# A decoder layer with a 32-expert mixture: three blocks of the first expert picked by TensorE instead of one or two, the routing tables built behind them, and the output projection's weights loaded in two halves

## What is computed

```python
xn = rms_norm(h, norm1_gain)
h = h + hybrid_mixer(xn, w_in, ...)              # ends in concatenate([h_m, h_g]) @ w_out
hn = rms_norm(h, norm2_gain)
logits = hn @ w_router + b_router
top_logit, top_idx = top_k(logits, 4)
gate = softmax(top_logit)
# for every expert e and each of its tokens:
hb = hn[tok] @ w_up[e] + b_up[e]                 # w_up[e] is 1024 x 2048
h_glu, h_lin = split(hb, 2)
h_glu = minimum(h_glu, 7); h_lin = clip(h_lin, -7, 7)
act = h_glu * sigmoid(1.702 * h_glu) * (h_lin + 1)
y[tok] += gate * (act @ w_down[e] + b_down[e])   # w_down[e] is 1024 x 1024
out = rms_norm(h + y, final_gain)
```

## Time and profile before

| | |
|---|---|
| median of three executions | 1283.21 us |
| the profiled execution: its time | 1281.32 us |
| the profiled execution: its span | 1279.5 us |
| TensorE matmuls busy | 1120.3 us, 88% |
| VectorE / ScalarE / GpSimd busy | 499.5 / 201.8 / 217.7 us |
| moved by DMA | 473.00 MB, 370 GB/s over the span |
| granted TensorE clock, mean | 0.951 of 2.4 GHz |

### The profile page before, as it was taken

The page is one execution under the profiler, slowest core; times in us unless marked ns, Lnnn a source line. Parts: engine busy times, 40 slices in busy tenths (PEclk is TensorE's granted clock), DMA queues, the critical chain, the costliest instruction groups (busy, mean ns, idle before and its releaser), DMA issues.

```text
span 1279.5 us, 28226 instructions
## 1 busy us (share of the span) xinstructions
PE 1120.3 (88%) x11061; PEld 508.3 (40%) x11062; DVE 499.5 (39%) x1234; ACT 201.8 (16%) x293; POOL 217.7 (17%) x385
## 2 busy tenths in 40 slices
PE   9999999989899888899989797989898979797750
PEld 5445554444344333334434343434343434343320
DVE  1393454673333342333333232333333323232317
ACT  2104321112111111111111111111111111111101
POOL 1000112001212221212222121212121212121112
PEclk9999999999999998989999898989898989898985
DMA  9308307669999999999999999999999999999996
GB/s 345 133 33 290 104 5 298 280 257 400 424 434 397 430 429 431 427 428 427 433 426 434 424 429 430 429 428 431 428 433 429 427 430 427 431 425 429 429 414 247
DMA packets 55636, 473.00 MB, mean 370 GB/s; under 512 B 7760, under 2 KB 25484, under 8 KB 41136
## 3 DMA queue, kind: packets, MB, share of 16 engines
q1 hardware_dynamic: 45608, 447.29, 83.6%
q0 software_dynamic: 7776, 20.46, 4.2%
q10 hardware_dynamic: 2216, 4.75, 1.0%
HBM read 447.43 MB, written 25.04 MB: 369 GB/s over the span
## 4 chain that ended last, share of the span: by engine, by line
PE 58%; DMA 34%; DVE 4%; issue 2%; SPq 1%; POOL 0%; ACT 0%; POOLq 0%; DVEq 0%; ACTq 0%
DMA W<-in_w_up_dram 30%; PE B L1601 27%; PE B L1286 11%; PE B L1618 11%; PE B L1441 4%; PE B L1320 2%; DMA hres<-misc,idx_s 2%; DMA yrow<-misc,idx_s 1%; DVE misc L1172 1%; DVE W L1248 1%; SPq L323 1%; DMA W<-in_w_in_dram 0%; DVE W L1249 0%; PE B L1394 0%; PE B L1374 0%
## 5 line engine op out<-in xcount | busy, mean ns | idle before, releaser
L1601 PE MATMUL B<-W,misc 128*32 128x512 f32 x4992 | 583.2, 617 | 108.7 <-DMA W<-in_w_up_dram 84.3
L1601 PEld LDWEIGHTS B<-W,misc 128*32 128x32 f32 x4992 | 183.3, 113 | 462.1 <-issue 454.7
L1618 PE MATMUL B<-W,misc 128*32 128x256 f32 x4992 | 287.7, 381 | 11.4 <-DVE misc L1198 8.7
L1618 PEld LDWEIGHTS B<-W,misc 128*32 128x32 f32 x4992 | 182.3, 111 | 134.7 <-issue 58.1
L1172 DVE TENSOR_TENSOR misc<-B,misc 128x512 f32<-128x512 f32 x77 | 53.3, 692 | 348.5 <-PE B L1601 348.5
L710 ACT ACTIVATE misc<-misc 128x256 f32<-128x256 f32 x78 | 32.5, 416 | 816.8 <-DVE misc L1174 816.8
L1286 PE MATMUL B<-W 128*128 128x512 f32 x320 | 140.2, 593 | 0.0
L526 POOL COPY idx_g<-idx_tab 128x1 uint32 (+1 forms) x77 | 14.3, 186 | 528.6 <-DVE misc L1203 519.6
L710 ACT ACT_TABLE_LOAD x78 | 100.1, 1283 | 5.7 <-DVE order_tab L1150 4.3
L538 POOL DMA_INDIRECT yrow<-misc,idx_s x75 | 75.1, 1001 | 135.0 <-DVE misc L1191 135.0
L1189 DVE TENSOR_TENSOR misc<-B,misc 128x256 f32<-128x256 f32 x78 | 33.1, 425 | 149.0 <-POOL idx_s L534 122.7
(11 more groups left out here) (296 smaller groups left out, 521.5 us busy)
## 6 DMA issues: line engine op xcount, KB each, us to landing
W<-in_w_up_dram SPq DMA_DIRECT2D x56, 4096.0 KB, 33.3
W<-in_w_down_dram SPq DMA_DIRECT2D x28, 4096.0 KB, 30.6
W<-in_w_up_dram SPq DMA_DIRECT2D x16, 2048.0 KB, 15.5
W<-in_w_down_dram SPq DMA_DIRECT2D x8, 2048.0 KB, 18.6
W<-in_w_in_dram SPq DMA_DIRECT2D x5, 2048.0 KB, 16.5
yrow<-W SPq DMA_DIRECT2D x1, 8192.0 KB, 40.4
W<-yrow SPq DMA_DIRECT2D x4, 2048.0 KB, 33.2
W<-in_x_dram SPq DMA_DIRECT2D x8, 512.0 KB, 7.0
```

Source lines behind the costliest of these rows:

```text
L1601: ins = mm(B[0][BT * j:BT * (j + 1), :].rearrange("p (g n) -> p g n", g=2), xT[:, BT * k:BT * (k + 1)], up(par)[:, k, :, QC * j:QC * (j + 1)],
L1618: ins = mm(B[5][BT * j:BT * (j + 1), 0:QC], aT[:, BT * q:BT * (q + 1)], down(par)[:, q, QC * j:QC * (j + 1)], start=(q == 0), stop=(q == N ...
```

## The change

The first `EARLY` = 3 blocks always belong to expert 0 and all have their rows picked by TensorE. Expert 0 is given at least three blocks; block 0 takes tokens of tiles 0 to 2 alone (`Mk_gap` moves tile 3's tokens behind place 31). So block 0 is picked while tile 3 still goes through the router. The up products of blocks 0, 1 and 2 run one after the other, block 1's into bank `B[3]` with its rows in `ysb` (`xT1`), and the small products of the ranks, the order and the token table stand between their `k` steps. The gate table, its spreading and `gate_tab` come behind the third up product, and then the down products of blocks 0 and 1. Filler products (`busy`) fall away. Pieces 2 and 3 of expert 1 are issued by ScalarE's queue instead of SyncE's. `w_out` is loaded in two halves by columns, so that piece 2 of expert 0 can be loaded once tile 3's first half of the projection is done.

```diff
+EARLY = 3
+NBMAX = T * TOPK // BT + NE + EARLY - 1
...
-            sp.dma_start(wo, w_out[0].rearrange("(k p) n -> p k n", p=P)).then_inc(s_wo, 16)
+            for n in range(2):
+                sp.dma_start(wo[n], w_out[0][:, 512 * n:512 * (n + 1)].rearrange("(k p) n -> p k n", p=P)).then_inc(s_wo, 16)
...
+            sp.wait_ge(s_out, 2 * NT - 1)
+            first(0, 2)
             sp.wait_ge(s_out, 2 * NT)
-            first(0, 2)
             first(0, 3)
...
             sp.wait_ge(s_hst, 16 * NT)
-            sp.wait_ge(s_picked, 2)
+            sp.wait_ge(s_picked, EARLY)
             first(0, 4)
-            sp.wait_ge(s_gtab, 1)
-            sp.wait_ge(s_trash, 16)
-            first(1, 2)
-            first(1, 3)
+            sp.wait_ge(s_tab, 1)
...
+            swish(0)
             act.wait_ge(s_ug, 1)
             act.activation(G32, G16, ACT.Copy).then_inc(s_g32, 1)
+            act.wait_ge(m_xg, 16)
+            act.wait_ge(m_u[3], 2)
+            act.wait_ge(s_gtab, 1)
+            for n in (2, 3):
+                load_piece(act, 1, n, slice(1, 2))
...
-            router_turn(NT - 1)
-            router_strips(NT - 1)
-            router_fold(NT - 1)
...
+            router_turn(NT - 1, [0])
             pe.wait_ge(s_pick, 1)
+            early_tile(0)
+            router_turn(NT - 1, [1])
+            early_tile(1)
+            router_strips(NT - 1, [0])
+            early_tile(2).then_inc(s_picked, 1)
+            router_strips(NT - 1, [1])
...
+            def between(g, k):
+
+                if (g, k) == (0, 0):
+                    router_fold(NT - 1)
+                elif (g, k) == (0, 3):
+                    counts()
+                elif (g, k) == (0, 6):
+                    late_rows()
+                elif (g, k) == (1, 4):
+                    order()
+                elif (g, k) == (2, 5):
+                    token_table()
...
-            expert(0, 0, 0, None)
+            block_up(0, 0, 16)
+            place_ranks()
+            pe.wait_ge(s_pick, 2)
+            pick_rows(1, range(NT)).then_inc(s_picked, 1)
+            place_turns()
+            pick_rows(2, range(NT)).then_inc(s_picked, 1)
+            bases()
+            block_up(1, 0, None)
+            block_up(2, 0, None)
+            gate_table()
+            spread_table(1, spread16, tok_s, 4)
+            spread_table(2, spread, gate_s, 6)
+            pe.wait_ge(s_tab, 1)
+            block_down(1, 0, 16)
+            block_down(2, 0, None)
+            more_blocks(0, 0, EARLY, base(1))
```

More of the change, by code:

```diff
@@ L1104, in _ @@
                 .then_inc(s_ranked, 1)
[L1106 to L1111, removed]
+            clamps(0)
+            picked_rows(2)
+            dve.wait_ge(s_place, 1)
+            link(V.tensor_copy(late[0:NE, 2:3], B[6][0:NE, 0:1]))
+            V.tensor_scalar(behind[0:NE, 0:NE + 1], iota_f[0:NE, 0:NE + 1], late[0:NE, 2:3], None, ALU.is_gt)
+            V.tensor_scalar(atp[0:NE, 0:NE], iota_f[0:NE, 0:NE], late[0:NE, 2:3], None, ALU.is_equal).then_inc(s_atp, 1)
+            gated(0)
+            dve.wait_ge(m_act, 1)
+            V.transpose(aT, z[:, 0:256]).then_inc(m_aT, 1)
             link(V.tensor_scalar(bbs[:, 0:NE], B[1][:, 0:NE], float(BT), None, ALU.mult))
@@ L1414, in rank_of @@
             def rank_of(c):
-                for d in range(c + 1):
-                    ins = mm(B[2][:, NE * c:NE * (c + 1)], stri16 if d == c else ones16, Mk16[:, d, :],
-                             start=(d == 0), stop=(d == c))
+                earlier = [(ones16, Mk16[:, d, :]) for d in range(c)]
+                if c == NT - 1:
+                    earlier.append((ones16, Mk_gap))
+                products = earlier + [(stri16, Mk16[:, c, :])]
+                for n, (lhs, rhs) in enumerate(products):
+                    ins = mm(B[2][:, NE * c:NE * (c + 1)], lhs, rhs, start=(n == 0), stop=(n == len(products) - 1))
                 return ins
@@ L1424, in ranks_early @@
                 for c in range(NT - 1):
-                    ins = rank_of(c)
+                    rank_of(c)
+                for d in range(NT - 1):
+                    ins = mm(B[2][:, P:P + 1], ones16, Mk16[:, d, 0:1], start=(d == 0), stop=(d == NT - 2))
                 ins.then_inc(s_cnt, 1)
@@ L1447, in project_out, with router_turn @@
                         cat(c + 1)
-            def router_turn(c):
-                if c >= 1:
-                    pe.wait_ge(s_nTe, 2 * c)
-                for hf in range(2):
+            def router_turn(c, halves=(0, 1)):
+                for hf in halves:
+                    if c >= 1 and hf == 0:
+                        pe.wait_ge(s_nTe, 2 * c)
                     pe.wait_ge(s_h, 2 * c + hf + 1)
@@ L1567, in spread_table, with block_up @@
                     .then_inc(s_spread, 1)
-            def between(k):
-                if k == 0:
-                    place_turns()
-                elif k == 1:
-                    bases()
-                elif k == 4:
-                    pe.wait_ge(s_pick, 3)
-                    pick_rows(1, range(NT)).then_inc(s_picked, 1)
-            busy(3)
-            pe.wait_ge(s_pick, 2)
-            pick_rows(0, range(NT - 1, NT)).then_inc(s_picked, 1)
-            busy(1)
-            late_rows()
-            busy(4)
-            place_ranks()
             def in_halves(loaded):
                 return isinstance(loaded, int) and loaded in (16, 32)
-            def block_up(g, par, before, loaded):
+            def between(g, k):
[9 more added lines that the diff above has]
+                    token_table()
+            def block_up(g, par, loaded):
+                early = isinstance(g, int)
+                out, rows = (B[3], xT1) if early and g == 1 else (B[0], xT)
                 pe.wait_ge(m_xT, g + 1)
-                if before:
+                if not early:
                     pe.wait_ge(m_z, g)
+                elif g > 0:
+                    pe.wait_ge(m_z, 1)
                 for k in range(NK):
@@ L1605, in block_up @@
                         ins.then_inc(m_u[k // 2], 1)
-                    if not before:
-                        between(k)
+                    if early:
+                        between(g, k)
             def block_down(g, par, loaded):
@@ L1621, in block_down, with more_blocks, token_table, gate_table @@
                         ins.then_inc(m_yh if q == 3 else m_y, 1)
+            def more_blocks(par, i, done, last):
+                with pe.If_lt(pe.to_reg(done), pe.to_reg(last)):
+                    with pe.Fori(done, last) as g:
+                        block_up(g, par, None)
+                        block_down(g, par, 16 * i + 16)
             def expert(par, i, first, last, out_first=False):
[L1625 removed]
                 if out_first:
                     block_down(first, 1 - par, 16 * i + 16 * par)
[L1628 to L1629 removed]
+                block_up(first, par, 16 * i + 16)
+                if not out_first:
                     block_down(first, 1 - par, 16 * i + 16 * par)
[L1631 to L1637 removed]
+                more_blocks(par, i, first + 1, last)
             def base(e):
[L1641 to L1643 removed]
+                return pe.value_load(base_tab[0:1, bass.ts(e, 1)], min_val=EARLY, max_val=NBMAX - 1)
+            def token_table():
                 pe.wait_ge(s_ug, 2)
                 table(UT16, G16, 5)
[L1647 removed]
+            def gate_table():
                 pe.wait_ge(s_ug, 3)
```

315 lines of the change are left out of this document (160 added, 155 removed).

## The result

| | median us | ratio, 95% interval |
|---|---|---|
| kernel before, 5 executions | 1285.04 | |
| changed kernel, 5 executions | 1292.12 | 1.0068 (1.0056 to 1.0080) |

The ratio comes with its own interval and is not the quotient of the two medians, which is 1.0055 (7.1 us). The profiled execution of the changed kernel took 1291.59 us, 10.3 more than that of before. The sign was forecast, the size was not: 0.68% of 1283 us are 8.7 us where I had 3.2, and 1292.12 lies outside the range of 1280.0 to 1288.7 that I gave.

A forecast was written before the change was run, and what follows sets the result against it. The DMA stream of expert weights was taken as the bound. Down-piece bytes from 329.0 instead of 325.5, plus 32.2, put the chain's piece near 361, 3.2 us later: 1283.2 + 3.2 = 1286.4 us, range 1280.0 to 1288.7.

The forecast's parts named there:

- The sign: Whole kernel: slower than before, by 3.2 us; this forecast case had a chance of 0.46.
- The front part: Up to the tables: up product 0 at 268.4, first reload at 290.5 (11.4 us earlier), last gate_tab copy ending at 298.7.
- VectorE's additional work: First three blocks: some 3 us of extra picking work, lying beside 24 us of TensorE.
- I take equal shares: SyncE's and ScalarE's queues share the rate equally, so piece 3 of expert 1 lands at 321.3.
- The stream stands still for 6.5 us.: Loads before the first down piece: six pieces in at 322.5, the down piece's bytes flow from 329.0.
- The chain's piece landed 32.2 later.: Piece 3 of the fourth expert lands 32.2 us after the first down piece's bytes begin, at 361.2.
- The PE-bound stretch behind it: Behind the chain's piece (DMA share 0.93 at 390 to 400 us): passes the shift on.
- The second rival: Expert 1's late piece comes in time, half the down product ending by 322: -2.0 to +2 us; chance 0.36.
- the faster one: ScalarE's queue gets more than its share or the table chain is shorter: -2.0 to -4 us; chance 0.18.
- The question how two queues share: Piece 3 of expert 1 lands at 311.0 if ScalarE's queue comes first, 322.5 if SyncE's does.
- One reading of the prediction: Kernel before, 300 to 305 us: DMA engines have no work, as pieces 2 and 3 of expert 1 are in.
- The count of twelve pieces instead of ten: From first reload to chain's piece: expert 1's two pieces join the ten; without a stop, 2 us earlier.

The follow-up runs named there:

- e3: The changed kernel with pieces 2 and 3 of expert 1 issued by SyncE's queue ahead of all reloads; ratio 1.0053 to the kernel before.
- e8: The kernel before with only pieces 2 and 3 of expert 1 moved behind the first two reloads; ratio 1.0077.
- e9: The changed kernel with expert 1's late pieces in SyncE's queue behind two reloads and the up products of blocks 1 and 2 interleaved; ratio 0.9984 to before.
- e7: The kernel before with only w_out loaded in two halves and piece 2 of expert 0 behind the first half; ratio 0.9995.
- e11: The changed kernel, late pieces still in ScalarE's queue, with the up products of blocks 1 and 2 interleaved; ratio 1.0042 to the kernel before.
- e6: e5 with six unused filler matmuls of 512 columns before block 3's up product; ratio 1.0003 to the kernel before.
- e10: e9 with the six filler matmuls of e6; ratio 0.9987 to the kernel before.
- e5: The changed kernel with late pieces in SyncE's queue behind two reloads and gate table and spreads inside block 2's up product; ratio 0.9994 to before.

## Why the prediction had the sign right and the size wrong

**Right.** Expert 0 had three blocks (78 blocks before and after). The front part came out to within 1 us: up product 0 at 268.0 for 268.4, first reload at 290.54 for 290.5, `gate_tab` at 298.0 to 298.25 for 298.7, `xT` of block 3 at 310.4 for 309.7. VectorE's additional work was covered: the trace has no wait of TensorE from 268.0 to 296.6 us. The two mechanisms were there: the late pieces of expert 1 stop block 3, and block 3 stops the stream. e3 and e8 show the accounting behind it from both sides, e9 that an early third up product does no harm once the late pieces have a good place in the queue, and e7 that the halves of `w_out` don't count.

**Wrong: the size of four terms, all low.**

1. "I take equal shares, with which it lands after four pieces and two gathers: 301.2 + 19.6 + 0.5 = 321.3." It landed at 324.2, with TensorE waiting from 316.4, and 1.1 us before the last of the six (issued at 304.75, 20.5 us to land). The sharing was as taken. The DMA queues from 302 to 322 us, q10 with ScalarE's loads, q1 with SyncE's, q0 with the gathers and scatters (packets, MB, share of the engines):

```profile
q10 hardware_dynamic: 269, 4.06, 47.8%
q1 hardware_dynamic: 280, 3.87, 45.8%
q0 software_dynamic: 165, 0.48, 6.1%
```

The two queues had equal shares within 5%. By 322 the packets of all but 0.03 of the 4.19 MB of ScalarE's two pieces had started, 20.8 us after 301.2, where the sum had 20.1. The other 2.2 us of the miss lie between there and the landing at 324.2. The sum had 2 us from the issue to the first bytes and put nothing between the start of the last packets and the landing. The term is 2.9 us short. (The 5.4 us per piece that I had read from ten pieces of before, and the 5.5 from six pieces here, 292.5 to 325.3, both hold such an end.)

2. "The stream stands still for 6.5 us." In slices of 0.7 us it is at full rate until 323 and again from 331.4, more than 8. The first down piece went out at 329.55 where I had 327.0.
3. "The chain's piece landed 32.2 later." The six pieces took 364.8 - 331.4 = 33.4. With the first two terms this makes the shift 7.1 for 3.2.
4. "The PE-bound stretch behind it ... passes a shift on." It added to it. Product by product, TensorE in the changed kernel:

```profile
364.93 3.39 PE L1654 MATMUL B<-W,misc 128*32 128x512 f32 x16 [2.50 <-DMA W<-in_w_up_dram]
368.13 3.64 PE L1671 MATMUL B<-W,misc 128*32 128x256 f32 x64
371.58 7.05 PE L1654 MATMUL B<-W,misc 128*32 128x512 f32 x64
378.45 3.64 PE L1671 MATMUL B<-W,misc 128*32 128x256 f32 x64
382.58 7.07 PE L1654 MATMUL B<-W,misc 128*32 128x512 f32 x64 [0.49 <-DVE misc L1228]
```

Before, the first of these took 1.92 us; here 3.39, and the block at 382.58 waited for its gathered rows. The fourth expert's five blocks end 9.6 us later than before, where they began 7.1 later. The whole span is 10.3 longer, and the ratio gives 8.7; single executions of before lie between 1281.3 and 1286.4, so the two agree.

The second rival, that the late piece comes in time, had 0.36 and is refuted by the wait of 7.97 us; the faster one too. The question how two queues share was left open between 311.0 and 322.5. The queues' bytes above settle it: equal shares, as the sum had them. With them the late piece lands near the end of all six pieces that were under way, at 324.2 in the changed kernel and 322.5 in e11. The Trainium skill, page "DMA: Bandwidth & Descriptors", section "Issuing engines are not separate DMA queues", says that issuing from several engines saves only the time to issue. The changed kernel agrees: with both queues busy, from 302 to 322 us, the engines moved 423 GB/s in all, no more than the 429 of one queue.

One reading of the prediction was wrong and did no harm to the sum. It says that at 300 to 305 us the DMA engines had no work, as pieces 2 and 3 of expert 1 were in. In the trace of before they landed 10.3 and 15.2 us after their issue, at 298.4 and 303.7, and the engines moved 417 GB/s from 288.5 to 301. The kernel before had hardly a hole there, only 3 us at 191 GB/s, so an earlier reload had little idle time to win. The count of twelve pieces instead of ten says the same, and that is why the sum was not touched.

## What to carry to other kernels

When a stream of loads is the bound, list the bytes that it must carry up to the next point where everything waits, and the holes before that point; a load that is made later is not free because an earlier one was won. Move the release of a buffer and you move what hangs behind it in the other queues. Read the price of a load from a stretch with the same other traffic, and add to a wait for weights the slower clock of the product behind it, here up to 1.7 us for 16 matmuls. Count a load until its landing and not until its last packets start, which made 2.2 us here.

## What the runs showed of the hardware

Two loads of 2 MB from a second queue were issued 7.8 us behind three others of the same size. From 302 to 322 us the two queues moved 4.06 and 3.87 MB, and the second of the two loads took 25.5 us and landed 1.1 us before the last of all six. 16 matmuls of 512 columns right behind a wait for weights took from 1.92 to 3.64 us, and the length of the wait alone didn't decide it: 3.39 after 2.50 us in the changed kernel, 1.92 after 2.32 before, and 2.88 after 1.63 and 1.92 after 3.12 in e6. Between 318 and 324 us, with TensorE idle, the granted clock of the changed kernel was 0.68 of 2.4 GHz on average and 0.75 in the next 6 us, that is, partly at 1.2 GHz. The fillers kept the clock up before one block (1.00 from 310 to 318 us in e6 and e10, 0.79 and 0.83 in e5 and e9) and were worth nothing in the time in both kernels that had them; in e6 the clock fell again at a later wait, in e10 it stays open where the gain went.
